# GpSimd's fourth sum of side weights, moved from the first to the third level of the triangle inversion

## The chip, the cores and the metric

One Trainium2 chip, one core of it. The metric is the device time of one execution in microseconds, median of the runs.

## What is computed

One step of a hybrid trunk on 128 context tokens and 1024 latent tokens, width 1024: a modulated RMSNorm, one combined input projection, two parallel mixers (pooling, and a bidirectional gated DeltaNet with 8 heads of 128), merge gates, an output projection, then an expert-choice mixture with 16 experts. The change lies in the DeltaNet part. Cut to what matters:

```python
proj = h @ w_in                      # q, k, v, gate of 8 heads, merge gates, pooling input
lmat = where(strict, (k_beta @ k.T) * decay, 0)       # per head, chunk and direction
a = lmat + eye
sol = triangular_solve(a, [v * beta, k_beta * exp(g)])
attn = (q @ k.T) * decay
def step(S, inp):                    # scan over the chunks
    v_new = u_c - w_c @ S
    o_c = q_c @ S + attn_c @ v_new
    S = S * d_c + k_c.T @ v_new
```

## The kernel before, in words

The eight heads run one after the other: heads 0 to 6 in a loop, head 7 written out after it. Each engine has its own program for a head (`body_pe`, `body_act`, `body_dve`, `body_pool`), and they meet through semaphores only. So the order of the work on an engine is the order of the code, and a wait holds up all that is queued behind it on that engine.

A head on TensorE is two things woven together. The first is the chain of the DeltaNet: products, transposes, the inversion of the triangles of both directions, a correction, and the scan over nine tiles. The second is side work (`project`): the columns of the input projection for the next head's q, k, v and gate, and two tiles of the side columns A and B. The side work is a row of jobs (`ORDER`) and `fill(place)` issues a fixed number of its steps at each place of the chain (`FILL`), so that TensorE has something to do while the other engines work on the chain. A step with 512 columns is the row `L823 MATMUL ... 128x512 f32 x2`.

A pair of side matrices, such as q and v ("qv"), is multiplied with a Strassen-like scheme: seven half-size jobs, "qv1" to "qv7" in the order 1, 2, 6, 7, 5, 4, 3, of four steps each. Some jobs use sums of halves of the weights. GpSimd makes them in `sums_first`, `sums_third` and `sums_fourth` (all recorded at L1303), and each one adds one to the semaphore `sums_ready`. The fourth sum of "qv" is written by `sums_fourth("qv")`: it waits until job "qv2" no longer reads the weights, and it is read by job "qv3". TensorE waits for it ahead of the first step of "qv3". In head 7 it is the fourth sum of "AB" instead, read by "AB3".

The inversion goes through six levels, `LEVELS = (2, 4, 8, 16, 32, 64)`, each over three groups of tiles g. TensorE: products Z (L1031), from the second level on each with a transpose X of the other triangle (L1023), then products P (L1031). VectorE in each level, in this order: `join(0)`, `to_low(0)`, `join(1)`, `to_up(0)`, `to_low(1)`, `join(2)`, `to_up(1)`, `to_low(2)`, `to_up(2)`. `join` is L1402 (copies from PSUM), `to_low` is L1409 and `to_up` is L1414 (both from SBUF to SBUF). TensorE's Z of the next level waits for `to_low` of its group and X for `to_up`. Between the groups stand the fills: one step at most places, none at P of group 2 in the second and third levels:

```python
FILL |= {f"{x}{b}_{g}": 0 if b in LEVELS[1:3] and (x, g) == ("P", 2) else 2 if (x, b, g) == ("P", 64, 2) else 1 for b in LEVELS for x in "ZP" for g in range(3)}
```

With these numbers "qv4" has its last step at P of group 0 in the third level, and "qv3" its first at P of group 1 there.

GpSimd's own row in a head (`body_pool`): seven sums, two masks of the decay (L1560), six masks of the triangles (L1567), the fourth sum, then for each direction d `low_part(d)` (L1574; waits for `to_up(2)` of level 2 for d = 0, of level 4 for d = 1) and `attention(d)` (L1581; one level later each), and at the head's end L1598 and L1600.

Of the kernel before, what the change touches and what calls it, by code (L numbers as in the profile page):

```python
# [78 lines left out]
def build(nc, a, out_p, out_s, out_sf, out_sb, dbg=None, stop=99):  # L79
    ctx = ExitStack()  # L80
    with ctx:
        sems = {}

        def sem(name):
            if name not in sems:
                sems[name] = ctx.enter_context(nc.semaphore(name))
            return sems[name]
# [536 lines left out]
        def drained_count(h, d, name, g):  # L624
            mine = [n for n in USES[d] if ((d, n) in BY_DVE) == ((d, name) in BY_DVE)]
            return h * (3 * len(mine)) + 3 * mine.index(name) + g + 1
# [6 lines left out]
        def all_drained(eng, h, d, name):  # L633

            eng.wait_ge(drained_sem(d, name), drained_count(h, d, name, 2))

        def alone(eng):

            eng.sem_inc(sem("waits_kept"), 1)
# [82 lines left out]
        def job_at(h, order, job):  # L722

            return order.index(job) + 1 if order is FIRST else len(FIRST) + len(ORDER) * h + order.index(job) + 1
# [26 lines left out]
        def weights_of(name):  # L751
            if name in MAT:
                return w_head[MAT[name]]
            return w_head[C_D[name]] if name in C_D else w_side["ABCDEF".index(name) % 2]
# [3 lines left out]
        def weights_wait(eng, h, order, name):  # L758

            if name in MAT:  # L760
                eng.wait_ge(sem(f"w_in{MAT[name]}"), 16 if order is FIRST else 16 * (h + (1 if name == "g" else 2)))
            elif name in C_D:
                eng.wait_ge(sem(f"w_in{C_D[name]}"), 16 * (h + 2))
            else:
                x = "ABCDEF".index(name)
                eng.wait_ge(sem(f"w_side_in{x % 2}"), 16 * (h + 1 + x // 4))
# [360 lines left out]
        def changed(h, lv, g):  # L1127
            return 3 * (len(LEVELS) * h + lv) + g + 1
# [168 lines left out]
        def sum_steps(eng, unit, h, order):  # L1297

            def sum_out(name, out, x, y, op):
                if name[-1] in "24":  # L1300

                    eng.wait_ge(sem("sums_ready"), summed_at(h, order, name[:2] + {"2": "1", "4": "2"}[name[-1]]))
                unit.tensor_tensor(out, x, y, op).then_inc(sem("sums_ready"), 1)  # L1303

            def sums_first(pair):

                for name in pair:
                    weights_wait(eng, h, order, name)
                one, two, to = weights_of(pair[0]), weights_of(pair[1]), sums_of(pair)
                sum_out(pair + "1", to[0], two[:, 0:KH, :], two[:, KH:KD, :], ALU.add)  # L1310
                sum_out(pair + "2", to[1], to[0], one[:, 0:KH, :], ALU.subtract)

            def sums_third(pair):

                one, two = weights_of(pair[0]), weights_of(pair[1])
                eng.wait_ge(sem("pj_filled"), job_at(h, order, pair + "c1"))
                sum_out(pair + "3", two[:, 0:KH, :], one[:, 0:KH, :], two[:, 0:KH, :], ALU.subtract)

            def sums_fourth(pair):

                one, to = weights_of(pair[0]), sums_of(pair)
                if pair != "kg":
                    eng.wait_ge(sem("pj_filled"), job_at(h, order, pair + "2"))
                sum_out(pair + "4", to[2], one[:, KH:KD, :], to[1], ALU.subtract)

            return sums_first, sums_third, sums_fourth
# [206 lines left out]
        def body_pool(pool, h, last_h=False):  # L1533
            order = ORDER_LAST if last_h else ORDER

            def gate_sums():

                w = weights_of("g")
                weights_wait(pool, h, order, "g")
                nc.gpsimd.tensor_tensor(w_sum2[0], w[:, 0:KH, :], w[:, KH:KD, :], ALU.add).then_inc(sem("sums_ready"), 1)  # L1540
                nc.gpsimd.tensor_scalar(w_sum2[1], w[:, 0:KH, :], -1.0, None, ALU.mult).then_inc(sem("sums_ready"), 1)

            sums_first, sums_third, sums_fourth = sum_steps(pool, nc.gpsimd, h, order)
            pool.wait_ge(sem("scan_done"), h + 1)
            pool.wait_ge(sem("pj_filled"), len(FIRST) + len(ORDER) * h)
            if last_h:
                gate_sums()
                sums_first("AB")
            else:
                sums_first("qv")  # L1550
                sums_first("kg")
                sums_fourth("kg")
                sums_third("qv")
                sums_third("kg")

            for d in range(2):
                sgn = 1 - 2 * d
                pool.wait_ge(sem("decay_exp"), 2 * h + d + 1)
                alone(pool)
                nc.gpsimd.affine_select(out=dm[d], in_=dm[d], compare_op=ALU.is_ge, fill=0.0, base=0,  # L1560
                                        pattern=[[0, NT], [sgn, P]], channel_multiplier=-sgn).then_inc(sem("decay_masked"), 1)

            for d in range(2):
                for g in range(3):
                    pool.wait_ge(sem("X_init"), 6 * h + 6)
                    alone(pool)
                    nc.gpsimd.affine_select(out=Yf[d][:, 3 * g:3 * g + 3, :], in_=Yf[d][:, 3 * g:3 * g + 3, :], compare_op=ALU.not_equal, fill=-1.0, base=0,  # L1567
                                            pattern=[[0, 3], [-1, P]], channel_multiplier=1).then_inc(sem("nl_masked"), 1)

            def low_part(d):  # L1570

                pool.wait_ge(sem("up_changed"), changed(h, 1 + 2 * d, 2))
                pool.wait_ge(sem("nL_ready"), 6 * h + 3 * d + 3)
                nc.gpsimd.tensor_tensor(nLlo[d], Yf[d], nL[d], ALU.subtract).then_inc(sem("nLlo_ready"), 1)  # L1574

            def attention(d):

                pool.wait_ge(sem("up_changed"), changed(h, 2 + 2 * d, 2))
                pool.wait_ge(sem("decay_masked"), 2 * h + d + 1)
                pool.wait_ge(sem("drained0_dve"), drained_count(h, 0, "kk", 2))  # L1580
                nc.gpsimd.tensor_tensor(attnT[d], kq[1], dm[d], ALU.mult).then_inc(sem("attn_ready"), 1)  # L1581

            if last_h:
                sums_third("AB")
            sums_fourth("AB" if last_h else "qv")
            all_drained(pool, h, 1, "kq")
            for d in range(2):
                low_part(d)
                attention(d)
            if last_h:  # L1590
                for pair, used in (("CD", "AB5"), ("EF", "CD5")):
                    pool.wait_ge(sem("pj_filled"), job_at(h, order, used))
                    sums_first(pair)
                    sums_third(pair)
                    sums_fourth(pair)
            for d in range(2):
                pool.wait_ge(sem(f"o_drained{d}"), (h + 1) * NT)
            nc.gpsimd.tensor_tensor(kq[0], kq[0], kq[1], ALU.add).then_inc(sem("o_added"), 1)  # L1598
            pool.wait_ge(sem("o_added"), h + 1)
            nc.gpsimd.tensor_tensor(kq[1], kq[0], kq[0], ALU.mult).then_inc(sem("o_squared"), 1)  # L1600
# [163 lines left out]
        @block.gpsimd  # L1764
        def _(pool):
            prologue_pool(pool)
            if stop >= 4:
                body_pool(pool, 0)
                with pool.Fori(1, H - 1) as h:
                    body_pool(pool, h)  # L1770
                body_pool(pool, H - 1, True)
            from_later["gpsimd"](pool)
# [1108 lines left out]
```

## Time and profile before

| | us |
|---|---|
| median of 3 runs | 2381.54 |
| lowest and highest run | 2379.71, 2381.61 |
| the profiled execution | 2380.56 |
| its span | 2378.8 |
| TensorE busy in it | 2297.4 |
| VectorE busy | 1110.7 |
| ScalarE busy | 928.5 |
| GpSimd busy | 372.8 |

The profiled execution's own time is 1.76 us longer than its span, and 0.98 us below the median of the runs. Busy times are of one execution; a matmul's end in the trace is modelled, so for TensorE it is safer to read the distance from one start to the next. PE is TensorE, DVE VectorE, ACT ScalarE, POOL GpSimd.

### The profile page before, as it was taken

How to read it: one execution, taken by the hardware profiler on the slowest of the kernel's cores; microseconds unless marked ns; L12 is line 12 of the kernel's file. 1: busy time of each engine (PE TensorE's matmuls, PEld its weight loads, DVE VectorE, ACT ScalarE, POOL GpSimd, SP SyncE). 2: the span in 40 equal slices, each digit the busy share in tenths (PEclk: the TensorE clock that was granted, in tenths of full speed). 3: DMA queues.
4: the chain of work that ended last, by engine and by line, in shares of the span. 5: the costliest groups of instructions: out<-in, count | busy, mean ns of one | idle time of the engine just before them, and what ended most of it. 6: DMA issues, size and time to landing. Idle time of an engine off the chain costs nothing.

```text
span 2378.8 us, 39734 instructions
## 1 busy us (share of the span) xinstructions
PE 2297.4 (97%) x14208; PEld 1681.5 (71%) x14208; DVE 1110.7 (47%) x2161; ACT 928.5 (39%) x2437; POOL 372.8 (16%) x270
## 2 busy tenths in 40 slices
PE   6999999999999999999999999779999999999997
PEld 3456666665756666665644444579999999999997
DVE  3587787868686877766336317710010000100003
ACT  4173746465563747465321133213222232222323
POOL 2040413122230404132100000000011100011101
PEclk9999999999999999999999999889999999999999
DMA  9710212120201202121442322368868888688885
GB/s 351 257 42 21 70 38 70 38 70 18 90 18 42 66 20 70 29 70 41 174 166 90 136 89 98 143 229 293 289 232 279 285 292 294 239 267 285 292 292 211
DMA packets 198882, 362.31 MB, mean 152 GB/s; under 512 B 9082, under 2 KB 72519, under 8 KB 195723
## 3 DMA queue, kind: packets, MB, share of 16 engines
q1 hardware_dynamic: 191994, 341.73, 41.2%
q0 software_dynamic: 6528, 19.47, 3.2%
q8 instruction: 36, 0.59, 0.1%
q14 instruction: 51, 0.42, 0.1%
q10 hardware_dynamic: 273, 0.11, 0.0%
HBM read 320.63 MB, written 40.65 MB: 152 GB/s over the span
## 4 chain that ended last, share of the span: by engine, by line
PE 91%; DVE 4%; DMA 2%; issue 1%; ACT 1%; SPq 0%; DVEq 0%; POOLq 0%; POOL 0%; ACTq 0%
PE bank L823 23%; PE bank L2537 21%; PE bank L2551 11%; PE bank L2150 5%; PE bank L1887 5%; PE bank L809 3%; PE bank L1031 2%; PE bank L801 2%; PE bank L1905 2%; PE bank L1023 2%; PE bank L1089 2%; PE bank L1100 1%; PE bank L1105 1%; PE bank L1016 1%; PE bank L1104 1%
## 5 line engine op out<-in xcount | busy, mean ns | idle before, releaser
L823 PE MATMUL bank<-arena 128*128 128x512 f32 x1344 | 679.5, 607 | 0.9
L2537 PE MATMUL bank<-arena 128*128 128x144 f32 x4096 | 512.6, 286 | 3.1 <-ACT arena L2571 3.1
L2537 PEld LDWEIGHTS bank<-arena 128*128 128x128 f32 x4096 | 509.3, 190 | 3.2 <-ACT arena L2571 3.2
L2644 DVE TENSOR_TENSOR arena<-arena,bank 128x144 f32<-128x144 f32 x128 | 39.1, 306 | 697.4 <-ACT arena L2585 697.4
L823 PEld LDWEIGHTS bank<-arena 128*128 128x128 f32 x1344 | 215.7, 191 | 87.9 <-issue 86.5
L2551 PE MATMUL bank<-arena 128*128 128x144 f32 x2048 | 257.3, 286 | 0.7 <-DVE arena L2644 0.7
L2551 PEld LDWEIGHTS bank<-arena 128*128 128x128 f32 x2048 | 253.8, 189 | 1.9 <-DVE arena L2644 0.9
L2585 ACT ACTIVATE arena<-bank 128x144 f32<-128x144 f32 x128 | 37.5, 293 | 460.5 <-PE bank L2537 460.5
L1031 PEld LDWEIGHTS bank<-arena 128*128 128x128 f16 x1296 | 97.1, 98 | 157.9 <-issue 139.8
L1209 ACT ACTIVATE arena<-bank 128x384 f16<-128x384 f16 (+1 forms) x360 | 159.7, 493 | 105.7 <-PE bank L1031 94.5
L1294 DVE SCALAR_TENSOR_TENSOR arena<-arena 128x1156 f32<-128x1156 f32 x96 | 150.1, 1563 | 1.3
L2150 PE MATMUL bank<-arena 128*128 128x512 f32 x288 | 128.7, 601 | 4.1 <-DVE arena L2044 2.1
L863 ACT ACTIVATE arena<-bank 128x128 f32<-128x128 f32 (+1 forms) x156 | 75.7, 490 | 129.1 <-PE bank L823 67.1
L1303 POOL TENSOR_TENSOR arena<-arena 128x512 f32<-128x512 f32 x68 | 94.9, 1404 | 167.9 <-DVE arena L1531 55.1
L1031 PE MATMUL bank<-arena 128*128 128x128 f16 x1296 | 120.8, 219 | 0.0
L1242 ACT ACTIVATE arena<-bank,arena 128x128 f32<-128x128 f32 x144 | 53.4, 371 | 160.8 <-PE bank L1089 160.8
L1887 PE MATMUL bank<-arena 128*128 128x512 f32 x256 | 110.6, 592 | 1.3 <-DVE arena L1510 1.3
L1402 DVE CAST_PREDICATED arena<-arena,bank 128x384 f16<-128x384 uint32 x144 | 79.7, 553 | 63.8 <-PE bank L1031 63.8
L2150 PEld LDWEIGHTS bank<-arena 128*128 128x128 f32 x288 | 53.8, 191 | 68.6 <-issue 66.4
L809 PEld LDWEIGHTS bank<-arena 128*128 128x128 f32 x768 | 92.3, 191 | 8.9 <-issue 6.2
L809 PE MATMUL bank<-arena 128*128 128x128 f32 x768 | 97.5, 276 | 0.0
L2597 ACT ACTIVATE arena<-bank,arena 128x128 f32<-128x128 f32 x128 | 47.2, 369 | 128.5 <-PE bank L2551 128.5
(327 smaller groups left out, 3071.3 us busy)
## 6 DMA issues: line engine op xcount, KB each, us to landing
arena<-in_exp_w_gate SPq DMA_DIRECT2D x32, 2048.0 KB, 10.2
arena<-in_exp_w_up SPq DMA_DIRECT2D x32, 2048.0 KB, 15.1
arena<-in_exp_w_down SPq DMA_DIRECT2D x32, 2048.0 KB, 10.8
arena<-in_w_in SPq DMA_DIRECT2D x52, 512.0 KB, 5.4
arena<-in_ada_w SPq DMA_DIRECT2D x24, 1024.0 KB, 8.1
side_dram<-arena SPq DMA_DIRECT2D x20, 576.0 KB, 4.2
arena<-g_dram SPq DMA_DIRECT2D x16, 576.0 KB, 4.2
arena<-in_x_sample SPq DMA_DIRECT2D x16, 512.0 KB, 5.8
```

The costliest lines, as they stand in the source:

```text
L809: ins = nc.tensor.matmul(bank[:, 0:CTX], weights_of(name)[:, k, :], hT3[:, k, 0:CTX], start=(k == 0), stop=(k == KD - 1))
L823: ins = nc.tensor.matmul(bank[:, 0:LH], w[:, k, :], x[:, k, :], start=(k == 0 and job[2] in "127"), stop=(k == KH - 1), skip_group_check=( ...
L863: nc.scalar.activation(result(h, order, name, span), bank[:, 0:SPAN[span][1]], ACT.Copy).then_inc(sem("pj_drained"), 1)
L1031: last = nc.tensor.matmul(TRI[d][g][:, i * P:(i + 1) * P], lhs[:, 3 * g + i, :], rhs[:, 3 * g + i, :], start=(n == 0), stop=(n == len(term ...
L1209: nc.scalar.activation(flat(dst, g), src[:, 0:384], ACT.Copy).then_inc(sem(f"drained{d}_act"), 1)
L1294: ins = nc.vector.scalar_tensor_tensor(conv_to[j][:, 0:CW], raw[j][:, tap:tap + CW], w, conv_to[j][:, 0:CW], ALU.mult, ALU.add)
L1303: unit.tensor_tensor(out, x, y, op).then_inc(sem("sums_ready"), 1)
L1402: nc.vector.copy_predicated(up[:, 3 * g:3 * g + 3, :], masks[:, 0, lv + 1, :].unsqueeze(1).to_broadcast([P, 3, P]), TRI[1][g][:, 0:384].re ...
L1887: last = nc.tensor.matmul(banks[n % RING][:, 0:CH], w_dn[half][:, k, col:col + P], bT3[:, k, CTX + c * CH:CTX + (c + 1) * CH], start=(k == ...
L2150: last = nc.tensor.matmul(banks[2 * (i % 2) + half][:, 0:512], mixT3[:, k, t * P:(t + 1) * P], w_outs[:, k, half * 512:(half + 1) * 512], ...
L2537: last = nc.tensor.matmul(banks[3 + f % 2][:, m * CAP:(m + 1) * CAP], w_unit[2 * half + m][:, k, col:col + P], xsT[:, k, :], start=(k == 0 ...
L2551: last = nc.tensor.matmul(banks[5 + dt % 2][:, 0:CAP], w_unit[4 + half][:, k, col:col + P], hid[:, k, :], start=(k == 0), stop=(k == KD - 1))
```

## The change

`sums_fourth` is called inside the loop over the two directions, behind the first `low_part`, in place of ahead of the loop. Nothing else is touched.

```diff
             if last_h:
                 sums_third("AB")
-            sums_fourth("AB" if last_h else "qv")
             all_drained(pool, h, 1, "kq")
             for d in range(2):
                 low_part(d)
+                if d == 0:
+                    sums_fourth("AB" if last_h else "qv")
                 attention(d)
```

On GpSimd, in the loop over heads 1 to 6 (L1567 masks of the triangles, L1303 the sum, L1574 `low_part`, L1578 the start of `attention`):

```order
 L1567 AFFINE_SELECT arena<-arena 128x384 [waits X_init] x6
-L1323 REGISTER_ALU
-L1302 REGISTER_ALU [waits pj_filled]
-L1303 TENSOR_TENSOR arena<-arena 128x512 [waits sums_ready]
 L635 REGISTER_ALU
 L1572 ISA [waits drained1_act]
 L1573 REGISTER_ALU [waits up_changed]
 L1574 TENSOR_TENSOR arena<-arena 128x1152 [waits nL_ready]
+L1323 REGISTER_ALU
+L1302 REGISTER_ALU [waits pj_filled]
+L1303 TENSOR_TENSOR arena<-arena 128x512 [waits sums_ready]
 L1578 ISA
```

The sum and its two register instructions stand behind `low_part`, whose wait (`up_changed`) they now pass first.

On TensorE nothing moves. This is its row in the third level, from the products P of group 1 to those of group 2; the L823 in the middle is the first step of "qv3", which reads the sum:

```order
L1050 REGISTER_ALU
L631 REGISTER_ALU [waits drained0_act]
L1031 MATMUL bank<-arena 128x128 [waits drained1_act]
L1031 MATMUL bank<-arena 128x128 x2
L747 REGISTER_ALU
L821 REGISTER_ALU [waits pj_added]
L823 MATMUL bank<-arena 128x512 [waits sums_ready]
L1050 REGISTER_ALU
L631 REGISTER_ALU [waits drained0_act]
L1031 MATMUL bank<-arena 128x128 [waits drained1_act]
L1031 MATMUL bank<-arena 128x128 x2
```

It stands the same before and after the change; what has moved is the instruction that raises `sums_ready` for it.

## Rows read from the trace of the kernel before

**Rows 1.** Page: busy time by engine, chain that ended last
```profile
PE 2297.4 (97%) x14208; PEld 1681.5 (71%) x14208; DVE 1110.7 (47%) x2161; ACT 928.5 (39%) x2437; POOL 372.8 (16%) x270
...
PE 91%; DVE 4%; DMA 2%; issue 1%; ACT 1%; SPq 0%; DVEq 0%; POOLq 0%; POOL 0%; ACTq 0%
```

**Rows 2.** Timeline, POOL: start us, us, engine, line, what, count
```profile
272.60 5.19 POOL L1567 TENSOR_SCALAR_AFFINE_SELECT arena<-arena 128x384 f32<-128x384 f32 x6 [6.31 <-DVE arena L1387]
277.76 1.27 POOL L1303 TENSOR_TENSOR arena<-arena 128x512 f32<-128x512 f32 x1
289.65 2.23 POOL L1574 TENSOR_TENSOR arena<-arena 128x1152 f16<-128x1152 f32 x1 [10.63 <-DVE arena L1414]
...
409.09 1.27 POOL L1303 TENSOR_TENSOR arena<-arena 128x512 f32<-128x512 f32 x1
```

**Rows 3.** Timeline, DVE and PE, head 1, first level into the second
```profile
277.82 0.33 PE L1031 MATMUL bank<-arena 128*128 128x128 f16 x3
277.92 1.52 DVE L1409 COPY_PREDICATED arena<-arena 128x384 f16<-128x384 uint32 x1
279.36 0.55 DVE L1402 CAST_PREDICATED arena<-arena,bank 128x384 f16<-128x384 uint32 x1
...
284.23 0.33 PE L1031 MATMUL bank<-arena 128*128 128x128 f16 x3
```

**Rows 4.** Timeline, DVE and PE, head 1, fifth level into the sixth
```profile
305.33 0.34 PE L1031 MATMUL bank<-arena 128*128 128x128 f16 x3
305.43 0.56 DVE L1409 COPY_PREDICATED arena<-arena 128x384 f16<-128x384 uint32 x1
...
311.26 0.33 PE L1031 MATMUL bank<-arena 128*128 128x128 f16 x3
```

**Rows 5.** Timeline, DVE and PE, head 1, third level into the fourth
```profile
291.92 0.56 DVE L1409 COPY_PREDICATED arena<-arena 128x384 f16<-128x384 uint32 x1 [0.15 <-DVE arena L1402]
291.98 1.07 PE L823 MATMUL bank<-arena 128*128 128x512 f32 x2
292.40 0.55 DVE L1402 CAST_PREDICATED arena<-arena,bank 128x384 f16<-128x384 uint32 x1
...
292.89 0.51 PE L1031 MATMUL bank<-arena 128*128 128x128 f16 x6
293.48 0.34 PE L1023 MATMUL bank<-arena 128*128 128x128 f16 x3
```

**Rows 6.** Timeline, POOL, DVE and PE, head 0, first level into the second
```profile
146.25 1.26 POOL L1303 TENSOR_TENSOR arena<-arena 128x512 f32<-128x512 f32 x1
146.70 0.33 PE L1031 MATMUL bank<-arena 128*128 128x128 f16 x3
146.81 1.12 DVE L1409 COPY_PREDICATED arena<-arena 128x384 f16<-128x384 uint32 x1
...
152.71 0.33 PE L1031 MATMUL bank<-arena 128*128 128x128 f16 x3
```

**Rows 7.** Timeline, POOL, DVE and PE, head 7, second level
```profile
1073.58 1.70 POOL L1303 TENSOR_TENSOR arena<-arena 128x512 f32<-128x512 f32 x1 [7.03 <-PE bank L823]
1073.59 0.56 DVE L1414 COPY_PREDICATED arena<-arena 128x384 f16<-128x384 uint32 x1
...
1075.84 0.33 PE L1031 MATMUL bank<-arena 128*128 128x128 f16 x3
...
1076.46 0.34 PE L1023 MATMUL bank<-arena 128*128 128x128 f16 x3 [0.28 <-DVE arena L1414]
```

**Rows 8.** Timeline, POOL, DVE and PE, head 7, third level
```profile
1082.96 2.23 POOL L1574 TENSOR_TENSOR arena<-arena 128x1152 f16<-128x1152 f32 x1 [7.68 <-DVE arena L1414]
...
1085.34 0.56 DVE L1409 COPY_PREDICATED arena<-arena 128x384 f16<-128x384 uint32 x1
1085.81 0.55 DVE L1402 CAST_PREDICATED arena<-arena,bank 128x384 f16<-128x384 uint32 x1
```

**Rows 9.** Windows, head 1, scan: us, busy PE, PEld, DVE, ACT, POOL, PEclk, DMA, GB/s
```profile
330.00:372.50 42.50, 42.39 (x243) 30.56 (x243) 26.81 (x49) 17.05 (x57) 3.78 (x2) 1.00 0.16 43
```

## The prediction

> **What bounds the kernel now.** I read the page first. TensorE is busy for 97% of the span, and 91% of the chain that ended last is its own [rows 1]. So the time moves only by what TensorE idles more or less; GpSimd, busy 16%, costs something only through those whom it holds up. I then read GpSimd's timeline for where the moved sum stands and what it stands near [rows 2], and the timelines of VectorE and TensorE around the old place [rows 3] and the new one [rows 5], beside a level with no GpSimd work near it [rows 4]. The heads repeat: the sum starts at 277.76 in head 1 and at 409.09 in head 2, 131.33 us later [rows 2]. Heads 0 and 7 differ and were read by themselves [rows 6 to 8].
>
> **What the sum costs where it is.** GpSimd's sum runs from 277.76 for 1.27 us, to 279.03 [rows 2]. VectorE's first `to_low` (L1409) starts inside it, at 277.92, and lasts 1.52 us, to 279.44 [rows 3]; with GpSimd silent the same instruction takes 0.56 [rows 4]. So it stood still for 0.96 us, and it ended 0.41 after the sum did. Head 0 repeats this: the sum ends at 147.51, L1409 at 147.93, 0.42 later [rows 6]. The next `join` (L1402) starts 0.33 after the sum's end (279.36) [rows 3]. These two distances are my rule for a blocked VectorE.
>
> What of this reaches TensorE: from the products P of group 1 to the first P of the next level it goes from 277.82 to 284.23, 6.41 us [rows 3]. The fifth level holds the same work, fill for fill, and takes from 305.33 to 311.26, 5.93 us [rows 4]. The old place therefore costs 0.48 us a head; the rest of the 0.96 lies beside the fill behind P of group 2. In head 0, where L1409 starts later in the sum and is held less (1.12), it is 152.71 - 146.70 = 6.01, so 0.08 [rows 6]. In head 7 the sum (of "AB") is already in the second level, and TensorE's last transpose starts 0.62 after the product before it (1075.84 to 1076.46) [rows 7]. Undisturbed it takes 0.17, the way other transposes follow a product that used up the fill: I take 0.45.
>
> Relief: 6 x 0.48 + 0.08 + 0.45 = **3.4 us**.
>
> **What it costs where it goes.** `low_part(0)` runs from 289.65 to 291.88 [rows 2]. The sum is behind it and is issued without a gap (in the first level it starts at 277.76 behind masks that end at 277.79) [rows 2], so it runs from about 291.85 to 293.12. Two things need what it holds.
>
> First, TensorE. The first step of "qv3" starts at 291.98 [rows 5] and waits for this very sum. It now comes at about 293.17 (0.05 for the semaphore), 1.19 late. Queued behind it are the step itself (0.91 to the next product, 291.98 to 292.89), P of group 2, and Z and X of the next level [rows 5]. There is no other fill to use, since P of group 2 has none here. From the step on to X: 0.91 + 0.17 + 0.17 = 1.25, so TensorE would be at X at 294.42, or up to 0.15 later if the weight load in front of the step no longer hides behind a matmul.
>
> Second, VectorE. Its L1409 starts at 291.92 [rows 5], 0.07 behind the sum, and is blocked until 293.12 + 0.41 = 293.53. The next L1402 then starts at 293.45 in place of 292.40 [rows 5]: 1.05 late. Everything up to X (L1414 ends, X starts: 293.48 - 292.40 = 1.08) keeps its distance, so X starts at 294.53 in place of 293.48 [rows 5].
>
> The two lie beside each other, VectorE's is a little later, and 1.05 us is the cost; were the weight load exposed, TensorE would be at X at 294.57, and VectorE's chain behind it would still set 1.05. All that follows in level and scan hangs on this point on TensorE, VectorE, ScalarE and GpSimd alike; in the scan TensorE is busy for 42.39 of 42.50 us [rows 9], at a granted clock of 1.00, so I see no slack that catches it. `attention(0)` waits for a `to_up` that comes four microseconds later and moves with it: it costs nothing of its own. So heads 1 to 6 pay 1.05 - 0.48 = 0.57 each, 3.4 together. For head 0 I take the same 1.05, less 0.08: 0.97.
>
> Head 7: `low_part(0)` ends at 1085.19, L1409 starts at 1085.34 and the next L1402 at 1085.81 [rows 8]. The sum would end at 1086.43, L1402 start at 1086.76: 0.95. Its reader "AB3" is two levels away, so only VectorE's block counts: 0.95 - 0.45 = 0.50.
>
> Sum: 3.4 + 0.97 + 0.50 = **+4.9 us**. Against the profiled execution's own 2380.56 that is 2385.4; the median of the runs lies 0.98 above it, which gives **2386.4**.
>
> The bounds of the new cost: below, 0, if the step of "qv3" were not the reader and VectorE got in first; above, the sum's whole 1.27 plus the 0.56 of a VectorE instruction in front of it, 1.83 a head. I am nearest to the blocked L1409 of rows 3, the same pair of instructions.
>
> **A rule and a row.** Which of the two gets in first is close: a lead of 0.07 us. In head 7 GpSimd started at 1073.58 and VectorE's L1414 at 1073.59, and VectorE was not slowed (0.56) while GpSimd took 1.70 in place of 1.27 [rows 7]. In head 1 GpSimd led by 0.16 and won. So a recorded lead of 0.01 loses, one of 0.16 wins, and 0.07 lies between. The Trainium skill, "SBUF — State Buffer", section "Who interferes with whom", says that a VectorE instruction with two SBUF inputs and a GpSimd instruction that reads SBUF exclude each other, and that issue order decides who blocks. Read on the recorded starts it gives the forecast, 2386.4; the row at 1073.58 breaks it by 0.01 us, so it doesn't settle the matter.
>
> **The rivals.**
>
> (a) *VectorE gets in first.* L1409 then ends at 292.48 as before, and the sum is pushed: in rows 7 it ended 1.13 after the VectorE instruction in front of it (1074.15 to 1075.28), so at 293.61. TensorE starts "qv3" at 293.66 or a little later and is at X at 294.91: 1.43 late, of which some 0.1 is won back, as VectorE is ahead there. With 1.33 in place of 1.05 in heads 0 to 6 (head 7's lead is 0.18, enough): 4.9 + 7 x 0.28 = +6.9, **2388.4**. For it: the row at 1073.58. Against: a longer lead. If the weight load is exposed too, about 0.1 more a head.
>
> (b) *The new place is covered, not slower than before.* GpSimd has the sum ready before its reader asks, at 291.98, and before VectorE's L1409 at 291.92. Then nobody waits for it and only the relief is left: -3.4, **2378.1**. For it: GpSimd idles much. Against: the sum would have to start by 290.7, in the midst of `low_part(0)`, and TensorE's row has the wait exactly there.
>
> (c) *The delay is caught later.* TensorE also waits on the others in the scan; if a wait there doesn't hang on the levels, it shrinks by what they are late, and the two changes about cancel: 0 to +2.5, middle **2382.8**. For it: 0.11 us of idle TensorE in the window of the scan, and more that modelled ends may hide. Against: each wait I find there is on VectorE or ScalarE in the same chain.
>
> (d) *More is lost*, by a collision of the moved sum with work that today runs free, another 0.3 us or more a head: 2389 to 2391. No row speaks for a particular one.
>
> **How the numbers follow.** Forecast 0.60, (a) 0.20, (b) 0.04, (c) 0.11, (d) 0.05. The forecast's own range is 2385.3 to 2387.5: the three runs before spread over 1.9 us. The 8 in 10 range takes in (a) and half of (c): 2383.2 to 2389.4. A difference of 0.2%, 4.8 us, is about what a measurement here can tell from none; the forecast of +4.9 lies on that bound, so half of it counts as the same. Slower: 0.31 + 0.19 + 0.05 = 0.55. Same: 0.29 + 0.01 + 0.11 + 0.02 of (b) = 0.43. Faster 0.02, the other half of (b), with noise.
>
> **What would show it.** In the first level L1409 is back at 0.56 and the four marks of rows 3 lie 5.93 apart in place of 6.41. In the third level GpSimd's L1303 starts right behind L1574 with 1.27; L1409 there takes 1.6, and TensorE's first L823 behind P of group 1 starts 1.2 later. The heads repeat at 131.33 + 0.57 = 131.90 us. Under (a) L1303 takes 1.7, L1409 stays at 0.56, and the period is 132.2. I am wrong if L823 starts on time there, if the period is below 131.33, or if the scan is shorter by what the levels are longer.

## The result, and the profile after

| | before | after |
|---|---|---|
| median, 10 runs each | 2381.38 | 2386.62 |
| lowest and highest | 2379.71, 2384.59 | 2385.93, 2390.37 |
| profiled execution, its span | 2380.56, 2378.8 | 2386.35, 2384.6 |

The change makes the kernel slower: ratio 1.0021, with a 95% interval of 1.0013 to 1.0029. The difference of the medians is 5.2 us; forecast was 4.9, as 2386.4. The interval spans 3.1 to 6.9 us, so it is partly luck that forecast and medians lie within 0.3 us of each other.

The page after, busy time and the chain that ended last (compare [rows 1]):

```profile
PE 2298.2 (96%) x14208; PEld 1682.1 (71%) x14208; DVE 1110.7 (47%) x2161; ACT 925.8 (39%) x2437; POOL 372.8 (16%) x270
...
PE 91%; DVE 3%; DMA 2%; issue 2%; ACT 1%; POOL 0%; SPq 0%; DVEq 0%; POOLq 0%; ACTq 0%
```

Nothing works more than before: 5.8 us of span, under 1 us of busy TensorE. The page can't say more, so the timeline has to. Head 1 of the kernel after, first level into the second, PE and DVE (start, us, engine, line, what):

```profile
279.70 0.33 PE L1031 MATMUL bank<-arena 128*128 128x128 f16 x3
279.80 0.57 DVE L1409 COPY_PREDICATED arena<-arena 128x384 f16<-128x384 uint32 x1
...
285.63 0.33 PE L1031 MATMUL bank<-arena 128*128 128x128 f16 x3
```

L1409 is back at 0.57, and between the two products P lie 5.93 us where [rows 3] had 6.41. That is the relief of 0.48 us. Third level of the same head, POOL, DVE and PE:

```profile
291.07 2.22 POOL L1574 TENSOR_TENSOR arena<-arena 128x1152 f16<-128x1152 f32 x1 [11.40 <-DVE arena L1414]
...
293.22 0.33 PE L1031 MATMUL bank<-arena 128*128 128x128 f16 x3
293.25 1.26 POOL L1303 TENSOR_TENSOR arena<-arena 128x512 f32<-128x512 f32 x1
293.34 1.60 DVE L1409 COPY_PREDICATED arena<-arena 128x384 f16<-128x384 uint32 x1 [0.15 <-DVE arena L1402]
294.57 1.12 PE L823 MATMUL bank<-arena 128*128 128x512 f32 x2 [1.02 <-POOL arena L1303]
294.85 0.55 DVE L1402 CAST_PREDICATED arena<-arena,bank 128x384 f16<-128x384 uint32 x1
295.31 0.55 DVE L1414 COPY_PREDICATED arena<-arena 128x384 f16<-128x384 uint32 x1
...
295.93 0.34 PE L1023 MATMUL bank<-arena 128*128 128x128 f16 x3
```

Both holds of the forecast are there at once. TensorE's step of "qv3" starts 1.35 us behind the product ahead of it, where a step otherwise follows after 0.17, and the row names GpSimd's sum as what it waited for. VectorE's L1409 takes 1.60 and ends at 294.94, 0.43 behind the sum; the next L1402 starts 0.34 behind it. X starts 2.71 behind the product P of group 1, and 0.07 behind the end of L1414 (295.86), as it does before (293.42 to 293.48).

The new wait also stands in the list of waits of PEld (TensorE's weight load), over head 1, in total, times, longest:

```profile
PEld bank L823 <- POOL arena L1303: 1.2, 1, 1.2
```

It was not in the list of before. Where the 5.8 us of span went, from the starts of GpSimd's rows in the two traces:

| stretch | before | after | more |
|---|---|---|---|
| start to the decay masks of head 0 (L1560) | 132.25 | 133.23 | 0.98 |
| from there to the last row of head 0 (L1600, now L1601) | 107.75 | 108.68 | 0.93 |
| six heads, 1 to 6 | 788.02 | 791.28 | 3.26 |
| head 7 | 143.38 | 143.85 | 0.47 |
| behind the heads | 1207.4 | 1207.56 | 0.16 |

The first row lies ahead of anything that the change touches; the executions of the experiments reach the same masks at 132.28 to 135.20, so I read it as scatter from one execution to the next. The change's own part is 0.93 + 3.26 + 0.47 = 4.7 us. The time of one head, taken over six of them, is 131.34 before and 131.88 after, and it is the finest gauge here: in each kernel below the heads repeat within some 0.02 us. It is called the period from here on.

### The profile page after: what moved, and what is told of

It reads as the page before. It is cut to its first block, busy times and chain, and to the rows that moved or that the text cites. A ratio compares the mean times of both kernels' runs of the same rounds, so it can differ in the third digit from the quotient of the medians.

```text
span 2384.6 us, 39734 instructions
## 1 busy us (share of the span) xinstructions
PE 2298.2 (96%) x14208; PEld 1682.1 (71%) x14208; DVE 1110.7 (47%) x2161; ACT 925.8 (39%) x2437; POOL 372.8 (16%) x270
## 4 chain that ended last, share of the span: by engine, by line
PE 91%; DVE 3%; DMA 2%; issue 2%; ACT 1%; POOL 0%; SPq 0%; DVEq 0%; POOLq 0%; ACTq 0%
PE bank L823 23%; PE bank L2538 21%; PE bank L2552 11%; PE bank L2151 5%; PE bank L1888 5%; PE bank L809 3%; PE bank L1031 3%; PE bank L801 2%; PE bank L1906 2%; PE bank L1089 2%; PE bank L1023 1%; PE bank L1100 1%; PE bank L1105 1%; PE bank L1016 1%; PE bank L1104 1%
## 5 line engine op out<-in xcount | busy, mean ns | idle before, releaser
L823 PE MATMUL bank<-arena 128*128 128x512 f32 x1344 | 679.5, 607 | 8.0 <-POOL arena L1303 7.1
L823 PEld LDWEIGHTS bank<-arena 128*128 128x128 f32 x1344 | 215.7, 191 | 96.0 <-issue 86.5
L1303 POOL TENSOR_TENSOR arena<-arena 128x512 f32<-128x512 f32 x68 | 95.3, 1411 | 161.0 <-DVE arena L1531 55.1
L1402 DVE CAST_PREDICATED arena<-arena,bank 128x384 f16<-128x384 uint32 x144 | 79.7, 553 | 68.2 <-PE bank L1031 68.2
```

Source lines behind the costliest of these rows:

```text
L823: ins = nc.tensor.matmul(bank[:, 0:LH], w[:, k, :], x[:, k, :], start=(k == 0 and job[2] in "127"), stop=(k == KH - 1), skip_group_check=( ...
L1402: nc.vector.copy_predicated(up[:, 3 * g:3 * g + 3, :], masks[:, 0, lv + 1, :].unsqueeze(1).to_broadcast([P, 3, P]), TRI[1][g][:, 0:384].re ...
```

## The experiments

The theory is the forecast's: a GpSimd instruction that reads SBUF and stands where VectorE's L1409 wants to start holds L1409, and L1409's delay is what TensorE loses. The late reader lies beside it. Rivals: the reader is the whole cost; the relief or the cost is caught later; the sum costs something wherever it stands.

| kernel | median | ratio to before (95%) | period |
|---|---|---|---|
| before | 2381.38 | | 131.34 |
| the change | 2386.62 | 1.0021 (1.0013 to 1.0029) | 131.88 |
| 1, sum left out | 2378.79 | 0.9986 (0.9977 to 0.9995) | 130.87 |
| 2, sum in the second level | 2378.31 | 0.9986 (0.9977 to 0.9995) | 130.85 |
| 3, VectorE's hold alone | 2387.24 | 1.0021 (1.0012 to 1.0030) | 131.88 |
| 4, the reader's wait alone | 2382.67 | 1.0007 (0.9998 to 1.0016) | 131.47 |
| 5, sum ahead of `low_part` | 2386.51 | 1.0021 (1.0011 to 1.0031) | 131.97 |
| 6, a short write first | 2386.85 | 1.0022 (1.0013 to 1.0032) | 131.94 |
| 7, a small sum first | 2388.49, one run | | 132.18 |

Each ratio is taken against runs of the kernel before that were made beside it: their median is 2381.38 for the change, 2382.10 for kernels 1 to 4 and 2381.77 for 5 to 7. So differences of a few tenths of a microsecond between rows are read from the period, not from the medians.

### 1. The fourth sum left out

In its place stands a sum of one column, written to a spare column of SBUF (`scratch`), so that the semaphore still counts. The side products that need the fourth sum come out without it. Cut to the lines that matter:

```diff
-            sums_fourth("AB" if last_h else "qv")
+            pool.wait_ge(sem("sums_ready"), summed_at(h, order, ("AB" if last_h else "qv") + "2"))
+            nc.gpsimd.tensor_tensor(scratch, h_sum1[:, 0, 0:1], h_sum2[:, 0, 0:1], ALU.add).then_inc(sem("sums_ready"), 1)
```

Expected:

> The fourth sum is left out in every head (job qv3, and AB3 in head 7, reads the weights without it); a sum of one column per partition stands in the old place. Theory (both places cost what they hold up on VectorE's shared access): the old place is freed and nothing is put in the new one, so the relief alone shows: 2.8 to 3.6 us faster than before (6 x 0.48 + 0.08 + 0.45 = 3.4), the heads repeat at 130.85 us in place of 131.33, and VectorE's first L1409 of a head takes 0.56. Rival (the relief is caught later in the scan, case c of the prediction): within 1 us of before, period 131.3.

The period is 130.87, 0.47 a head under before, and the time is lower by 0.14%, 3.3 us. So the old place did cost the 0.48 us that was read between TensorE's marks, in full, and nothing catches it later in the head.

### 2. The sum in a hole of VectorE

```diff
+            pool.wait_ge(sem("up_changed"), changed(h, 0, 2))
             sums_fourth("AB" if last_h else "qv")
```

Expected:

> The fourth sum waits for the last to_up of the first level, so it runs while VectorE idles ahead of the first join of the second level (2.2 us of idling in the trace after the change), and is ready some 6 us ahead of its reader. Theory: it costs nothing there, so the same as with the sum left out: 2.8 to 3.6 us faster than before, period 130.85, GpSimd's L1303 1.27 and every L1409 of the first three levels 0.56. Rival (any place costs something, since the sum holds VectorE's joins too): about as before, period 131.2 or more.

Head 1, GpSimd and VectorE:

```profile
282.90 1.27 POOL L1303 TENSOR_TENSOR arena<-arena 128x512 f32<-128x512 f32 x1 [4.45 <-DVE arena L1414]
...
284.90 0.56 DVE L1402 CAST_PREDICATED arena<-arena,bank 128x384 f16<-128x384 uint32 x1 [2.23 <-PE bank L1031]
285.60 0.56 DVE L1409 COPY_PREDICATED arena<-arena 128x384 f16<-128x384 uint32 x1
```

The whole sum, with the same result for the reader, ends at 284.17, 8 us ahead of its reader (the expectation had some 6) and inside the 2.23 us in which VectorE waits for TensorE. Period 130.85, as with the sum left out: in this place it is free. This kernel computes everything and is faster than before by 0.14% (interval 0.05 to 0.23) and than the change by 8 us. It is the version to keep: the same instruction, held back by one wait.

### 3. VectorE's hold without the late reader

On top of 2, so that the reader's sum is ready long before; a sum of the same size that nobody reads goes to the new place:

```diff
                 low_part(d)
+                if d == 0:
+                    pool.wait_ge(sem("qd_ready"), 2 * h + 2)
+                    nc.gpsimd.tensor_tensor(qT[:, 0:512], h_sum1[:, 0, :], h_sum2[:, 0, :], ALU.add)
                 attention(d)
```

Expected:

> As e2, and in the new place, behind low_part(0), a sum of the same size that nobody reads (128x512 f32, two inputs from SBUF). So TensorE finds its sum on time and only VectorE's L1409 is held. Theory: VectorE's chain alone sets the delay, so the whole cost of the new place shows: 1.05 us a head over e2, 7 x 1.05 + 0.95 = 8.3 us over e2 and 4.9 over before; L1409 takes 1.6, TensorE's step of qv3 starts on time. Rival (the late reader is what costs, VectorE's block is hidden behind fills): within 1.5 us of e2.

Head 1, third level:

```profile
293.13 0.33 PE L1031 MATMUL bank<-arena 128*128 128x128 f16 x3
293.16 1.27 POOL L1592 TENSOR_TENSOR arena<-arena 128x512 f32<-128x512 f32 x1
293.25 1.60 DVE L1409 COPY_PREDICATED arena<-arena 128x384 f16<-128x384 uint32 x1 [0.15 <-DVE arena L1402]
293.30 1.07 PE L823 MATMUL bank<-arena 128*128 128x512 f32 x2
...
294.90 0.35 PE L1031 MATMUL bank<-arena 128*128 128x128 f16 x3 [0.35 <-DVE arena L1409]
...
295.83 0.34 PE L1023 MATMUL bank<-arena 128*128 128x128 f16 x3 [0.59 <-DVE arena L1414]
```

The step of "qv3" starts on time, 0.17 behind its product, and TensorE waits later instead: ahead of Z for L1409, ahead of X for L1414. X starts 2.70 behind the product, where the change has 2.71, and the period is that of the change to the hundredth. VectorE's hold alone is enough for the whole cost of the new place: 131.88 - 130.85 = 1.03 us a head. The added wait on `qd_ready` only makes sure that `qT` is free to be written; it delays nothing, since the sum starts at 293.16 and `low_part(0)` ends at 293.20.

### 4. The late reader without VectorE's hold

On top of 2: two writes of zeros behind `low_part(0)`, of which the second raises the semaphore that `low_part(0)` raised before, and TensorE's first step of "qv3" waits for it. Cut to the lines that matter; `low_part(0)` itself no longer raises the semaphore:

```diff
+                if d == 0:
+                    pool.wait_ge(sem("qd_ready"), 2 * h + 2)
                 low_part(d)
+                if d == 0:
+                    nc.gpsimd.memset(qT[:, 0:512], 0.0)
+                    nc.gpsimd.memset(qT[:, 512:1024], 0.0).then_inc(sem("nLlo_ready"), 1)
...
+                        if job == "qv3":
+                            pe.wait_ge(sem("nLlo_ready"), 2 * h + 1)
```

Expected:

> As e2, and behind low_part(0) GpSimd writes zeros twice (128x512 f32 each, no input), and TensorE's first step of qv3 waits for the second. Nothing on GpSimd reads SBUF there. Theory: the wait of the reader costs by itself what puts its X behind the old time: start of the step + 1.30 (0.96 to the next product, 0.34 to X) less the old 1.50 between the undisturbed step and X. With the two writes taking 1.2 us together that is 1.0 us a head and +7 over e2; for each 0.1 us that they take less, 0.1 less, and nothing below 0.25. L1409 stays at 0.56, if what only writes does not hold VectorE (the Trainium skill, SBUF — State Buffer, Who interferes with whom). Rival (only VectorE's access counts, reader's wait is covered): as e2. Rival on the rule: L1409 is held here too, and ends some 0.4 after the writes.

Head 1, third level (this kernel's L1411 is L1409 of the others, its L825 their L823, its L1025 their L1023):

```profile
293.13 0.53 POOL L1597 MEMSET arena<- 128x512 f32 x1
293.24 0.56 DVE L1411 COPY_PREDICATED arena<-arena 128x384 f16<-128x384 uint32 x1 [0.15 <-DVE arena L1404]
293.59 0.53 POOL L1598 MEMSET arena<- 128x512 f32 x1
...
294.25 1.12 PE L825 MATMUL bank<-arena 128*128 128x512 f32 x2 [0.79 <-POOL arena L1598]
...
295.55 0.33 PE L1025 MATMUL bank<-arena 128*128 128x128 f16 x3
```

L1411 keeps its 0.56 under both writes: they only write, and they don't hold it. (The Trainium skill, "SBUF — State Buffer", "Who interferes with whom", says that two SBUF inputs on VectorE contend with a GpSimd instruction that reads SBUF, not with one that only writes; by that rule, the trace agrees.) The writes took 0.99 us together, not 1.2, and X starts 1.30 behind the step, as expected. X is late by 0.76: it starts 2.43 behind the product of group 1 (293.12), in kernel 2 1.67 (292.00 to 293.67). The period is only 0.62 over that of 2, since VectorE runs ahead here and a later stall shrinks: the X of the next group follows its product after 0.18 (296.63 to 296.81), where in kernel 2 it waited for VectorE's L1414 and followed after 0.30 (294.77 to 295.07). The semaphore of `low_part(0)` comes later here too, but its own reader stands behind all six levels.

So a late reader costs too, by itself, and in the change it is covered by VectorE's hold, but not by much. There the step starts 1.35 behind its product, not 1.13 as here; with the 1.30 from step to X, TensorE alone would be at X 2.65 behind the product, 0.98 late. With the same 0.14 won back that is an estimate of 0.84 us a head for the reader alone, against 1.03 for the hold. Taking only the hold out of the change would save about 0.2 us a head; both have to go.

### 5. Sum and `low_part(0)` in the other order

```diff
-            sums_fourth("AB" if last_h else "qv")
             all_drained(pool, h, 1, "kq")
             for d in range(2):
+                if d == 0:
+                    pool.wait_ge(sem("up_changed"), changed(h, 1, 2))
+                    sums_fourth("AB" if last_h else "qv")
                 low_part(d)
```

Expected:

> In the third level the sum and low_part(0) change places: both wait for the last to_up of the second level, the sum goes first. So the sum is ready 1 us ahead of its reader, and low_part(0) (2.2 us) now stands where the sum stood. Theory (what costs in the third level is whatever GpSimd instruction holds VectorE's first L1409, not the sum as such): low_part ends where the sum ended, L1409 ends 0.41 later, X is late by the same 1.05 and the total is the one of the change, +4.9 over before, period 131.9, L1409 1.6, TensorE's step of qv3 on time. Rival (the sum's lateness is what costs): the relief stays and nothing is lost, -3.3, period 130.85.

Head 1, third level:

```profile
290.79 1.27 POOL L1303 TENSOR_TENSOR arena<-arena 128x512 f32<-128x512 f32 x1 [11.47 <-DVE arena L1414]
...
292.02 2.22 POOL L1574 TENSOR_TENSOR arena<-arena 128x1152 f16<-128x1152 f32 x1
...
292.98 1.68 DVE L1409 COPY_PREDICATED arena<-arena 128x384 f16<-128x384 uint32 x1 [0.15 <-DVE arena L1402]
293.04 1.07 PE L823 MATMUL bank<-arena 128*128 128x512 f32 x2
```

The sum is ready at 292.06, well ahead of its reader at 293.04. Now it is `low_part(0)` that holds L1409 (1.68), and the time is that of the change. The period is 0.09 above that of the change, as L1409 is held a little longer and X starts 2.78 behind its product (292.87 to 295.65). So the sum itself is not at fault: two GpSimd instructions in a row behind `to_up(2)` are 3.4 us long, and whichever is second stands under L1409.

### 6 and 7. Who gets in first

Kernel 6 is the change with one short write between `low_part(0)` and the sum, kernel 7 with a sum of one column there (`scratch` is the spare column again; its definition is cut):

```diff
                 if d == 0:
+                    nc.gpsimd.memset(scratch, 0.0)
                     sums_fourth("AB" if last_h else "qv")
```

```diff
                 if d == 0:
+                    nc.gpsimd.tensor_tensor(scratch, h_sum1[:, 0, 0:1], h_sum2[:, 0, 0:1], ALU.add)
                     sums_fourth("AB" if last_h else "qv")
```

Expected of 6:

> The change with a memset of one column (0.1 us) between low_part(0) and the sum. In the trace of the change the sum starts 0.09 us ahead of VectorE's L1409 and wins; here it starts at about the same time or 0.01 behind. Theory (whoever asks first holds, with little difference between the two engines' start records): VectorE wins as in head 7 of the kernel before, L1409 takes 0.56, the sum 1.7, the reader starts 1.6 to 1.7 late and X 1.35 to 1.45; the period is 132.2 to 132.3 and the whole 2 us or more over the change (+7 over before). Rival (GpSimd's instruction behind another keeps its hold): L1409 1.7, period 132.0, +5.5 over before.

Expected of 7:

> As e6 with a sum of one column (0.18 us, two inputs) in place of the memset, so that the big sum starts some 0.08 us behind VectorE's L1409. Theory: VectorE wins clearly, L1409 0.56 to 0.7, the sum 1.65 to 1.75, period 132.2 to 132.4. Rival: L1409 1.7 or more, the sum 1.27.

Kernel 6, head 1, third level (its L1410 is L1409 of the others):

```profile
295.26 0.10 POOL L1590 MEMSET arena<- 128x1 f32 x1
295.32 1.26 POOL L1304 TENSOR_TENSOR arena<-arena 128x512 f32<-128x512 f32 x1
295.37 1.63 DVE L1410 COPY_PREDICATED arena<-arena 128x384 f16<-128x384 uint32 x1 [0.15 <-DVE arena L1403]
```

The expectation missed: the write moved the sum by some 0.04 us only, since it starts inside the end of the instruction ahead of it and the sum inside its own. A lead of 0.05 is left and GpSimd still wins. The numbers are those of the expectation's rival (a GpSimd instruction behind another keeps its hold), but as GpSimd still led, this run doesn't tell the two apart; kernel 7 does. Kernel 7, the same place (L1410 and L1415 are `to_low` and `to_up`):

```profile
293.77 0.19 POOL L1590 TENSOR_TENSOR arena<-arena 128x1 f32<-128x1 f32 x1
293.86 0.57 DVE L1410 COPY_PREDICATED arena<-arena 128x384 f16<-128x384 uint32 x1 [0.15 <-DVE arena L1403]
293.92 1.62 POOL L1304 TENSOR_TENSOR arena<-arena 128x512 f32<-128x512 f32 x1
294.33 0.55 DVE L1403 CAST_PREDICATED arena<-arena,bank 128x384 f16<-128x384 uint32 x1
294.80 1.16 DVE L1415 COPY_PREDICATED arena<-arena 128x384 f16<-128x384 uint32 x1
295.59 1.13 PE L824 MATMUL bank<-arena 128*128 128x512 f32 x2 [1.52 <-POOL arena L1304]
```

Here VectorE leads by 0.06 and wins: L1410 keeps 0.57, the sum takes 1.62, the reader starts 1.68 late. The sum stood behind another instruction here too and lost, so kernel 6's rival is out. The join (L1403), whose data come from PSUM, keeps its 0.55 under the sum, while L1415, with its data in SBUF, is held. The period is 132.18, from one run, in which all six heads agree within 0.02. This is the prediction's rival (a), made on purpose, and it came out at its price: 131.34 - 0.48 + 1.33 = 132.19. In head 7 of the same run GpSimd leads by 0.06 (1092.29 to 1092.35) and wins, L1410 taking 1.63. With the row at 1073.58 in [rows 7] the leads of GpSimd read 0.05 and 0.06 win, 0.01 and -0.06 lose.

## Why the prediction was right, point by point

- **The relief.** Forecast 0.48 a head from [rows 3] against [rows 4]; kernel 1 measures 0.47, kernel 2 0.49, with 3.3 us on the whole for 3.4. The comparison of two levels with the same fills was the step that carried it: L1409 stood still for 0.96 us, and half of that lay beside a fill. No kernel here changes the fills, so that split is read from the rows, not tested.
- **The cost in the new place.** Forecast 1.05 a head by VectorE's chain, with the reader's wait beside it and a little shorter. Measured 1.03, and kernels 3 and 4 show the two parts singly: 1.03 for the hold, 0.62 for a step that starts 0.96 us late (1.13 behind its product in place of 0.17). The exposed weight load, for which the forecast allowed up to 0.15, cost 0.05: 1.30 from step to X for 1.25. The forecast's "the two lie beside each other" holds: together they cost what the larger one does.
- **Heads 0 and 7.** Forecast 0.97 and 0.50, measured 0.93 and 0.47. The parts fit too: the relief is 0.07 and 0.47 by kernel 2 (forecast 0.08 and 0.45), the cost 1.02 and 0.91 by kernel 3 over 2 (forecast 1.05 and 0.95).
- **The sum.** 4.7 us by the traces for a forecast of 4.9, 5.2 by the medians. The traces are the better test of the forecast, since it was added up head by head. The half microsecond between the last two is not told apart from scatter: the executions profiled differ by up to 3 us before the first head's masks.
- **The tie.** The lead is 0.09 us, not the 0.07 forecast (L1409 at 293.34, sum at 293.25), and GpSimd won, in all heads. That it won was not shown by any row at the time: between a lead of 0.01 that lost and one of 0.16 that won, 0.07 was a guess, given 0.60 against 0.20, and that it fell this way was in part luck. Kernel 6 shows afterwards that 0.05 is enough. The rule read on recorded starts was wrong by a few hundredths at most.
- **Rival (a)** was priced right (kernel 7: X 1.49 late with 0.16 won back, for a forecast of 1.43 and 0.1), but it left out that `to_up(0)` (L1415 there) is then held in L1409's stead, 1.16 in place of 0.56. It costs nothing more only because the late reader already covers it. The trace of before has the same in head 7, behind the L1414 that won:

```profile
1074.06 1.63 DVE L1409 COPY_PREDICATED arena<-arena 128x384 f16<-128x384 uint32 x1
```

- **Rival (b)** did not happen in the change; kernel 2 shows that it was to be had one level earlier. The forecast looked for a hole in the third level only.
- **Rival (c)** fell with kernel 1: the relief arrives at the end in full. A delay of TensorE alone is caught in small part (0.14 of 0.76 in kernel 4), one of VectorE's chain is not (1.03 of the 1.04 by which X is late in the change, 2.71 against 1.67). **Rival (d)** had no row and no case.

## What to carry to other kernels

A short GpSimd instruction that reads SBUF can have a cost, and it is read from the VectorE instruction on SBUF data that starts inside it: compare its duration and the distance between TensorE's marks with the same stretch elsewhere in the trace where GpSimd is silent. Before it is moved, two things are looked up at the new place: when VectorE is idle there for the instruction's whole length, and when the reader asks. The best place tried here was neither the first nor the third level but VectorE's 2.2 us of waiting between the first and the second, reached by one wait on VectorE's own progress.

## What the runs showed of the hardware that was not expected

- The recorded starts tell who holds whom to within a few hundredths: GpSimd with a lead of 0.05 us won, with 0.01 it lost.
- A held L1409 ended 0.41 to 0.43 us behind the GpSimd instruction in every case read, though it takes 0.56 alone.
- A memset on one column behind a GpSimd instruction took 0.10 us by its row and pushed what follows by about 0.04.
- TensorE's step started 0.06 us behind the end of the sum that it waited for (294.51 to 294.57), and 0.13 behind the end of a memset (294.12 to 294.25).
- A join, which takes its data from PSUM, was not held: 0.55 (L1403 at 294.33 in kernel 7) inside the same sum that held L1415.
